# Later sum over partitions, and another order of entries in the two block-product GEMMs

## The chip, the cores and the metric

The kernel runs on one core of a Trainium2 chip, as one program. The metric is the time of one execution in microseconds on the device; the number that counts is the median of the runs. A core has a matrix engine (TensorE, PE in the profile), a vector engine (VectorE, DVE), a scalar engine (ScalarE, ACT), a general engine (GpSimd, POOL) and a queue engine (SyncE, SP). Each runs its own instructions in the order in which the program lists them, and waits on semaphores that the others raise.

## The reference

A stack of blocks on 512 tokens of 1024 features, all in float32: a bidirectional gated delta net with an MLP, a dilated window attention with an MLP, a final RMS norm, and then two more blocks (a Fourier and long-convolution mixer with a convolved feed-forward net on tokens and context, and a latent attention with such a feed-forward net on the 512 tokens). The change touches the GEMMs that follow a norm:

```
h = rmsnorm(x, g)            # x * rsqrt(mean(x^2) + eps) * g
mlp:       x + relu(h @ w1)**2 @ w2
conv ffn:  gate, val = split(modulate(h) @ w_up)
           x + g2 * (silu(dwconv3(gate)) * val) @ w_down
```

## The kernel before, in words

Features lie on the 128 partitions, 8 tiles of them (KD), and tokens along the free axis. Weights come in chunks of 128 x 1024, four in a ring. A product of float32 accuracy is made of three matmuls: ScalarE rounds a chunk to a high part (`split_high`, L208), GpSimd subtracts to get the low part (`split_low`, L214), and PE multiplies low by high, high by low and high by high (L278 to L280). There are two slots for high and low parts, so the split of chunk n waits until tile n - 2 is done. An output tile n takes chunk n: 24 matmuls of 512 columns, or 48 of 256, and one of four PSUM banks.

`LateNorm`: the GEMM starts on x times the gain, and the division by the root mean square is made when VectorE drains a tile. On ScalarE stand, in this order (`split_high_first`): the high parts of x (`high`), the split of chunk 1, the squares (`square`, L474), the split of chunk 2, the root (`root`, L375), and then the splits from chunk 3 on. VectorE adds the squares of the eight tiles (`add_squares`, L362), PE adds them over the partitions with a matmul of ones (`tensor`, L371), ScalarE takes the root, VectorE inverts it (`inverse`, L505 or L3212) and can then drain tile 0. `multiply_tiles` issues PE's part, with L371 behind tile 1. One stream runs in the stages gdn_in, window_in and mlp1 (`mlp_stage`), two in mix_in, ffn0, mla_in and ffn1. The stages follow one another with a barrier between.

`mlp_seven_stage` (mlp0) and `ffn_seven_stage` (ffn1) make the first output tiles in the plain way (six in mlp0, `WHOLE`; ten in ffn1, five gate and value pairs), and the rest in pairs j of two weight chunks by `SevenProducts`: seven products of half-size blocks (G1, G0, V1, S1, S2, S4, S3), 12 matmuls of 256 columns each, on weights G, V and their sums S and on token blocks (b10, b00, b11 plain; T1, T2, T4, T3 differences, called mixes). Every block and every weight sum needs a high part from ScalarE and a low part (`rest`, `low_sum`, `low_raw`, `low_s3`) from VectorE or GpSimd. PE's order in pair j is G1, G0, V1, S1, the S3 of pair j - 1, S2, S4. S2 adds into the bank of G0, so it waits until VectorE has read it out (`add_c11`, L3163), and S1, S2, S4 wait for their low parts on VectorE (`low_sum`, L3157). In pair 0, PE also waits for the remainders of the blocks (`ready`), and pair 1 waits for all of them. The order of each engine's entries in this turn from tiles to products is written out by hand.

```
for n in range(min(RING, g.whole)):
    tile(n, n, 0)
    if n == 1 and norm.late:
        norm.tensor(pe)
```

## Time and profile before

| | us |
|---|---|
| median of 3 runs | 3236.82 (3236.43 to 3240.74) |
| the profiled execution, its own time | 3245.98 |
| its span, first to last instruction | 3244.2 |
| PE busy | 3046.9 (94%) |
| VectorE, GpSimd, ScalarE busy | 1720.5, 1208.2, 1156.6 |

The mean clock that PE was granted is 0.963 of full speed; it has two levels, 1.2 and 2.4 GHz. Times in rows are microseconds from the start of the span. A duration of a matmul overlaps the next one's, so the distance between starts is what a matmul costs.

### The profile page before, as it was taken

The numbers are of one execution on the slowest core, as the hardware profiler recorded it, in microseconds if no ns is written. First come the engines' busy times: TensorE is split into PE (matmuls) and PEld (weight loads), VectorE is DVE, ScalarE is ACT, GpSimd is POOL, SyncE is SP. The second block draws the span as 40 slices with busy tenths as digits, with TensorE's granted clock in tenths as the row PEclk, the third lists the DMA queues.
The fourth block names the chain that finished last, engine by engine and source line by source line (L and its number), as shares of the span: only waits on it lengthen the run. The fifth ranks groups of instructions, "written<-read, shape, count | busy, mean of one in ns | idle before, by whom it ended". The sixth has DMA issues, their size and how long they took to land. (4 is left out here: it accounts for less than half of the span.)

```text
span 3244.2 us, 51107 instructions
## 1 busy us (share of the span) xinstructions
PE 3046.9 (94%) x19422; PEld 2460.3 (76%) x19422; DVE 1720.5 (53%) x2594; ACT 1156.6 (36%) x1905; POOL 1208.2 (37%) x642
## 2 busy tenths in 40 slices
PE   8988888999999989999898999999999979999998
PEld 6845666998878767888477788888888545589987
DVE  7835653762131535311577766555556666478731
ACT  4323433563231723222221332222223435345632
POOL 4432213664434024444122022222232147646643
PEclk9978989999999989999899999999999989999999
DMA  4326443222324022332212012122121112122322
GB/s 146 97 75 219 151 159 117 97 105 89 95 90 116 20 63 93 97 94 95 86 59 80 30 59 65 58 65 65 58 65 59 50 38 49 39 78 92 106 97 84
DMA packets 80218, 275.75 MB, mean 85 GB/s; under 512 B 9500, under 2 KB 12380, under 8 KB 79291
## 3 DMA queue, kind: packets, MB, share of 16 engines
q1 hardware_dynamic: 79771, 273.27, 26.2%
q8 instruction: 107, 1.75, 0.2%
q14 instruction: 52, 0.43, 0.0%
q10 hardware_dynamic: 288, 0.30, 0.0%
HBM read 263.54 MB, written 2.12 MB: 82 GB/s over the span
## 5 line engine op out<-in xcount | busy, mean ns | idle before, releaser
L214 POOL TENSOR_TENSOR weights_low<-weight_ring,weights_high 128x1024 fp32r<-128x1024 f32 x303 | 750.4, 2477 | 1441.0 <-ACT weights_high L208 1441.0
L208 ACT ACTIVATE weights_high<-weight_ring 128x1024 fp32r<-128x1024 f32 x317 | 333.9, 1053 | 631.3 <-PE bank L280 627.3
L278 PE MATMUL bank<-ffn_in_high,weights_low 128*128 128x512 f32 (+2 forms) x1176 | 399.0, 339 | 6.4 <-POOL weights_low L214 3.8
L279 PE MATMUL bank<-ffn_in_low,weights_high 128*128 128x512 f32 (+2 forms) x1176 | 398.5, 339 | 0.0
L280 PE MATMUL bank<-ffn_in_high,weights_high 128*128 128x512 f32 (+2 forms) x1176 | 398.2, 339 | 0.0
L278 PEld LDWEIGHTS bank<-ffn_in_high,weights_low 128*128 128x128 f32 x1176 | 222.9, 190 | 32.3 <-POOL weights_low L214 4.4
L279 PEld LDWEIGHTS bank<-ffn_in_low,weights_high 128*128 128x128 f32 x1176 | 223.0, 190 | 24.5
L280 PEld LDWEIGHTS bank<-ffn_in_high,weights_high 128*128 128x128 f32 x1176 | 222.0, 189 | 24.2
L634 DVE TENSOR_TENSOR mlp_down_low<-mlp_hidden,mlp_down_high 128x512 fp32r<-128x512 f32 x64 | 48.8, 764 | 285.3 <-ACT mlp_down_high L553 285.3
L278 PE MATMUL bank<-mlp_down_high,weights_low 128*128 128x512 f32 x496 | 193.1, 389 | 2.0 <-POOL weights_low L214 2.0
L279 PE MATMUL bank<-mlp_down_low,weights_high 128*128 128x512 f32 x496 | 193.0, 389 | 0.0
L280 PE MATMUL bank<-mlp_down_high,weights_high 128*128 128x512 f32 x496 | 192.9, 389 | 0.0
L634 DVE TENSOR_TENSOR ffn_in_low<-ffn_hidden,ffn_in_high 128x512 fp32r<-128x512 f32 (+1 forms) x44 | 61.3, 1416 | 142.5 <-ACT ffn_in_high L553 142.5
L553 ACT ACTIVATE mlp_down_high<-mlp_hidden 128x512 fp32r (+1 forms) x64 | 40.2, 631 | 231.0 <-PE bank L280 225.8
L278 PEld LDWEIGHTS bank<-mlp_down_high,weights_low 128*128 128x128 f32 x496 | 93.1, 188 | 21.9 <-issue 2.4
L280 PEld LDWEIGHTS bank<-mlp_down_high,weights_high 128*128 128x128 f32 x496 | 93.1, 188 | 19.2
L279 PEld LDWEIGHTS bank<-mlp_down_low,weights_high 128*128 128x128 f32 x496 | 93.1, 188 | 19.2
L278 PE MATMUL bank<-gdn_in_high,weights_low 128*128 128x512 f32 x248 | 98.6, 398 | 0.5 <-POOL weights_low L214 0.5
L278 PE MATMUL bank<-mlp_in_high,weights_low 128*128 128x512 f32 x248 | 97.3, 393 | 0.8 <-POOL weights_low L214 0.8
L280 PE MATMUL bank<-gdn_in_high,weights_high 128*128 128x512 f32 x248 | 98.1, 395 | 0.0
L279 PE MATMUL bank<-gdn_in_low,weights_high 128*128 128x512 f32 x248 | 98.1, 395 | 0.0
L279 PE MATMUL bank<-mlp_in_low,weights_high 128*128 128x512 f32 x248 | 96.5, 389 | 0.0
(791 smaller groups left out, 7905.3 us busy)
## 6 DMA issues: line engine op xcount, KB each, us to landing
weight_ring<-in_mod SPq DMA_DIRECT2D x96, 512.0 KB, 4.7
weight_ring<-in_ffn_up SPq DMA_DIRECT2D x88, 512.0 KB, 3.5
weight_ring<-in_mlp_up SPq DMA_DIRECT2D x64, 512.0 KB, 3.5
weight_ring<-in_mlp_down SPq DMA_DIRECT2D x64, 512.0 KB, 3.4
weight_ring<-in_ffn_down SPq DMA_DIRECT2D x44, 512.0 KB, 3.5
weight_ring<-in_gdn_in SPq DMA_DIRECT2D x32, 512.0 KB, 3.5
weight_ring<-in_dswa_in SPq DMA_DIRECT2D x27, 512.0 KB, 3.5
weight_ring<-in_fh_in SPq DMA_DIRECT2D x16, 512.0 KB, 3.4
```

What stands on the lines that cost most here:

```text
L208: act.activation(self.high[:, (g.s0 + at) % SPLIT, 0:g.floats], raw, ACT.Copy).then_inc(self.high_ready, 1)
L214: pool.tensor_tensor(self.low[:, slot, 0:g.floats], self.ring[:, (g.c0 + at) % RING, 0:g.floats], self.high[:, slot, 0:g.floats], ALU.subt ...
L278: pe.matmul(bank, wl, ah, start=start, stop=False)
L279: pe.matmul(bank, wh, al, start=False, stop=False)
L280: return pe.matmul(bank, wh, ah, start=False, stop=stop)
L553: last = act.activation(self.high[at % 2][:, :, lo:lo + tokens], src(k * self.kc, self.kc), ACT.Copy)
L634: last = dve.tensor_tensor(self.low[at % 2][:, :, lo:lo + tokens], src(k * self.kc, self.kc), self.high[at % 2][:, :, lo:lo + tokens], ALU ...
```

## The change

With one stream, L371 is issued behind tile 2 instead of tile 1 (also in mlp0's own code); with two streams it stays. In mlp0, ScalarE makes the squares before the split of chunk 1, and the high parts of S1, S2 and S4 in a row before it keeps product G1 (`keep_b`); VectorE makes the mix T1, then the inverse, then T2 and T4, while T3 goes to GpSimd; the weight sums stand behind tile 3 instead of tile 5, and pair 0's `add_c11` right behind the low parts of S1 and S2. In ffn1 the remainder of b00 moves from behind pair 3 to behind pair 2, that of T2 from VectorE to GpSimd, GpSimd makes the raw low parts of pair 0 before its remainders, and pair 0's `add_c11` stands ahead of the low part of S2. With `late_sums`, ffn1 keeps the wait of the sum S2 for the high part of S1, and mlp0 loses it.

```diff
--- before.py
+++ after.py
@@ -311,7 +311,7 @@
             norm.tensor(pe)
         for n in range(min(RING, g.whole)):
             tile(n, n, 0)
-            if n == 1 and norm.late:
+            if n == (1 if len(streams) > 1 else 2) and norm.late:
                 norm.tensor(pe)
         if beside:
             beside.tensor(pe)
@@ -2929,7 +2929,7 @@
     BLOCKS_OF = ("b10", "T4", "b00", "T1", "T2", "b11", "T3")
     UNIT = KH * P
 
-    def __init__(self, core, name, g, ctx, wide, first, pairs, blocks_high, blocks_low, kept, s3, banks, slots=None):
+    def __init__(self, core, name, g, ctx, wide, first, pairs, blocks_high, blocks_low, kept, s3, banks, slots=None, late_sums=False):
         self.core, self.g, self.pairs, self.wide = core, g, pairs, wide
         g.seven = self
         self.bh, self.bl = blocks_high, blocks_low
@@ -2945,7 +2945,7 @@
             w[self.S2], w[self.S4] = halves(shared, 1 - slot)
         self.sums = dict(zip((self.S1, self.S2, self.S4), [core.ps[b] for b in banks]))
         self.base = 2 * (first % 2)
-        self.s3, self.kept = s3, kept
+        self.s3, self.kept, self.late_sums = s3, kept, late_sums
 
     def signals(self, sems):
         (self.raw_high, self.raw_low, self.s_sums, self.s_high, self.s_low, self.s3_sum, self.s3_high, self.s3_low, self.products,
@@ -3075,7 +3075,7 @@
     def high_sum(self, act, j, w):
 
         self.slot_free(act, j, w)
-        act.wait_ge(self.s_sums, 3 * j + (3 if w != self.S1 else 2 if j else 1))
+        act.wait_ge(self.s_sums, 3 * j + (3 if w != self.S1 else 1 if self.late_sums and not j else 2))
         act.activation(self.wh[w], self.sums[w][:, :], ACT.Copy).then_inc(self.s_high, 1)
 
     def high_s3(self, act, j):
@@ -3137,7 +3137,7 @@
         dve.wait_ge(self.s_sums, 3 * j + 1)
         if j:
             dve.wait_ge(self.s_low, 3 * j - 1)
-        else:
+        elif self.late_sums:
             dve.wait_ge(self.s_high, 1)
         dve.tensor_tensor(self.sums[self.S2][:, :], self.sums[self.S1][:, :], self.raw(dve, j, False)[:, 0:self.UNIT], ALU.subtract) \
            .then_inc(self.s_sums, 1)
@@ -3252,6 +3252,9 @@
             def _(pool):
                 core.split_low(pool, up, up.ahead, WHOLE)
                 seven.low_raw(pool, 0)
+                pool.wait_ge(tokens_scaled, KD)
+                pool.wait_ge(mixed_ready, len(MIXES) - 1)
+                pool.tensor_tensor(raw["T3"], quarter(1, 1), quarter(0, 1), ALU.subtract).then_inc(mixed_ready, 1)
                 seven.sum_s3(pool, 0)
                 for j in range(N):
                     if j + 1 < N:
@@ -3302,8 +3305,9 @@
 
                 first_tile()
                 tile(1)
+                tile(2)
                 norm.tensor(pe)
-                for n in range(2, WHOLE):
+                for n in range(3, WHOLE):
                     tile(n)
                 for j in range(N):
                     if j == 1:
@@ -3340,8 +3344,8 @@
                 if not up.ahead:
                     core.split_high(act, up, 0, 0, 0)
                 norm.high(act)
+                norm.square(act)
                 core.split_high(act, up, 1, 1, 0)
-                norm.square(act)
                 core.split_high(act, up, 2, 2, 0)
                 scale_tokens()
                 norm.root(act)
@@ -3351,14 +3355,12 @@
                         round_block(MIXES[n - 3])
                 for w in (seven.G1, seven.G0, seven.V1):
                     seven.high_raw(act, 0, w)
-                seven.high_sum(act, 0, seven.S1)
+                for w in (seven.S1, seven.S2, seven.S4):
+                    seven.high_sum(act, 0, w)
                 for j in range(N + 2):
                     now, later = j < N, j + 1 < N
                     if now:
                         seven.keep_b(act, j)
-                    if j == 0:
-                        for w in (seven.S2, seven.S4):
-                            seven.high_sum(act, 0, w)
                     if later:
                         seven.high_raw(act, j + 1, seven.G1)
                     if j >= 2:
@@ -3395,9 +3397,8 @@
                 dve.sem_inc(up_drained, RING)
 
                 def mix(which):
-                    first, second = dict(T1=(quarter(0, 1), quarter(0, 0)), T2=(quarter(1, 1), raw["T1"]), T4=(quarter(1, 0), raw["T2"]),
-                                         T3=(quarter(1, 1), quarter(0, 1)))[which]
-                    if which in ("T2", "T4"):
+                    first, second = dict(T1=(quarter(0, 1), quarter(0, 0)), T2=(quarter(1, 1), raw["T1"]), T4=(quarter(1, 0), raw["T2"]))[which]
+                    if which != "T1":
                         dve.wait_ge(mixed_ready, MIXES.index(which))
                     dve.tensor_tensor(raw[which], first, second, ALU.subtract).then_inc(mixed_ready, 1)
 
@@ -3425,19 +3426,21 @@
                 norm.lows(dve)
                 norm.sums(dve, order)
                 dve.wait_ge(tokens_scaled, KD)
-                for which in MIXES:
-                    mix(which)
+                mix("T1")
                 norm.inverse(dve, order)
+                mix("T2")
+                mix("T4")
                 for n in range(WHOLE):
-                    if n == WHOLE - 1:
-                        seven.sum_s1(dve, 0)
                     tile(n)
                     if n < len(MIXES) - 1:
                         rest(MIXES[n])
-                seven.low_sum(dve, 0, seven.S1)
-                seven.sum_s2(dve, 0)
-                seven.sum_s4(dve, 0)
-                seven.low_sum(dve, 0, seven.S2)
+                    if n == WHOLE - 3:
+                        seven.sum_s1(dve, 0)
+                        seven.sum_s2(dve, 0)
+                        seven.sum_s4(dve, 0)
+                for w in (seven.S1, seven.S2):
+                    seven.low_sum(dve, 0, w)
+                seven.add_c11(dve, 0, hid[:, WHOLE, 0:H])
                 for j in range(N + 1):
                     now, later = j < N, j + 1 < N
                     gates, values = [hid[:, WHOLE + 2 * (j - 1) + x, :] if j else None for x in range(2)]
@@ -3451,7 +3454,7 @@
                         rectify(WHOLE + 2 * (j - 1), seven.c12_added, j)
                     if later:
                         seven.sum_s2(dve, j + 1)
-                    if now:
+                    if now and j:
                         seven.add_c11(dve, j, hid[:, WHOLE + 2 * j, 0:H])
                     if later:
                         seven.sum_s4(dve, j + 1)
@@ -3499,7 +3502,7 @@
         kept = core.xc[:, 0:6, :]
         last = 6 + (FIRST - 1) % 2
         seven = SevenProducts(core, "ffn1_seven", up, ctx, H, FIRST, N, block_high, block_low, kept, pick[:, :, :].rearrange("p a n -> p (a n)"),
-                              (13 - last, last, 5), [f[:, KH * H:KH * H + SevenProducts.UNIT] for f in flat])
+                              (13 - last, last, 5), [f[:, KH * H:KH * H + SevenProducts.UNIT] for f in flat], True)
         rows = RowsGemm(core, "ffn1_down", down, [(tiles_of(hid, 0, T), core.x, T, mod.gate(1, 0))], ctx, 2,
                         both=[t[:, :, 0:H].rearrange("p k t -> p (k t)")[:, 0:2 * T].rearrange("p (b k t) -> p b k t", b=2, k=1) for t in parts[0]])
         GATE = core.ps[4]
@@ -3516,8 +3519,8 @@
             MIXES = ("T1", "T2", "T4", "T3")
             PLAIN = ("b10", "b00", "b11")
             ROUNDED = (*PLAIN, *MIXES)
-            RESTS = ("b10", "b00", "T4", "T1", "T2", "T3")
-            POOL_RESTS = ("b11",)
+            RESTS = ("b10", "b00", "T4", "T1", "T3")
+            POOL_RESTS = ("T2", "b11")
             index = SevenProducts.BLOCKS_OF.index
 
             @block.sync
@@ -3542,10 +3545,10 @@
                 core.split_low(pool, up, 8, 9)
                 mix("T4")
                 core.split_low(pool, up, 9, up.whole)
+                seven.low_raw(pool, 0)
                 for name in POOL_RESTS:
                     pool.wait_ge(block_rounded, ROUNDED.index(name) + 1)
                     pool.tensor_tensor(block_low[index(name)], blocks[name], block_high[index(name)], ALU.subtract).then_inc(pool_rests, 1)
-                seven.low_raw(pool, 0)
                 mix("T3")
                 seven.sum_s3(pool, 0)
                 for j in range(N):
@@ -3747,16 +3750,17 @@
                             scale_tokens(k)
                     if m == 2:
                         rest("b10")
+                        rest("b00")
                     if m == FIRST - 2:
                         dve.wait_ge(hidden_ready, FIRST - 1)
                         seven.sum_s1(dve, 0)
-                        for name in ("b00", "T4", "T1"):
+                        for name in ("T4", "T1"):
                             rest(name)
                 seven.low_sum(dve, 0, seven.S1)
                 dve.wait_ge(hidden_ready, FIRST)
                 seven.sum_s2(dve, 0)
                 seven.sum_s4(dve, 0)
-                rest("T2")
+                seven.add_c11(dve, 0, gate_halves(0)[0])
                 seven.low_sum(dve, 0, seven.S2)
                 for j in range(N + 1):
                     now, later = j < N, j + 1 < N
@@ -3770,7 +3774,7 @@
                         more_taps(j - 1)
                     if later:
                         seven.sum_s2(dve, j + 1)
-                    if now:
+                    if now and j:
                         seven.add_c11(dve, j, gate_halves(j)[0])
                     if later:
                         seven.sum_s4(dve, j + 1)
```

## Rows read from the trace of the kernel before

**Rows 1.** The page: span, busy time of each engine.

```profile
span 3244.2 us, 51107 instructions
...
PE 3046.9 (94%) x19422; PEld 2460.3 (76%) x19422; DVE 1720.5 (53%) x2594; ACT 1156.6 (36%) x1905; POOL 1208.2 (37%) x642
```

**Rows 2.** The list of PE's waits, whole run (engine, line, releaser: total us, times, longest).

```profile
PE bank L604 <- ACT mixer_out_high L553: 4.4, 1, 4.4
...
PE bank L371 <- DVE mlp_hidden L362: 3.3, 2, 1.8
```

**Rows 3.** PE's timeline, window_in, 928 to 932 us (start, duration, instruction [idle before]).

```profile
928.48 0.39 PE L280 MATMUL bank<-window_in_high,weights_high 128*128 128x512 f32 x1
930.62 1.12 PE L371 MATMUL bank<-window_qkv,ones 128*128 128x512 f32 x2 [1.75 <-DVE window_qkv L362]
...
931.81 0.39 PE L279 MATMUL bank<-window_in_low,weights_high 128*128 128x512 f32 x1
```

**Rows 4.** ScalarE's timeline, window_in: root, split of chunks 3 and 4.

```profile
931.78 0.69 ACT L375 ACTIVATE rstd<-bank,eps 128x512 f32<-128x512 f32 x1 [6.67 <-PE bank L371]
932.37 1.05 ACT L208 ACTIVATE weights_high<-weight_ring 128x1024 fp32r<-128x1024 f32 x1
937.38 1.06 ACT L208 ACTIVATE weights_high<-weight_ring 128x1024 fp32r<-128x1024 f32 x1 [3.96 <-PE bank L280]
```

**Rows 5.** GpSimd's timeline, window_in: lower parts of chunks 2 and 3.

```profile
925.18 3.57 POOL L214 TENSOR_TENSOR weights_low<-weight_ring,weights_high 128x1024 fp32r<-128x1024 f32 x1 [2.14 <-ACT weights_high L208]
933.49 2.42 POOL L214 TENSOR_TENSOR weights_low<-weight_ring,weights_high 128x1024 fp32r<-128x1024 f32 x1 [4.74 <-ACT weights_high L208]
```

**Rows 6.** ScalarE's timeline, mlp0: the squares, now behind the split of chunk 1.

```profile
563.62 3.70 ACT L474 ACTIVATE mlp_hidden<-x 128x2048 f32<-128x2048 f32 x2
```

**Rows 7.** GpSimd's timeline, mlp0: lower parts of chunks 1 and 2.

```profile
563.79 2.40 POOL L214 TENSOR_TENSOR weights_low<-weight_ring,weights_high 128x1024 fp32r<-128x1024 f32 x1 [9.51 <-ACT weights_high L208]
568.34 3.57 POOL L214 TENSOR_TENSOR weights_low<-weight_ring,weights_high 128x1024 fp32r<-128x1024 f32 x1 [2.15 <-ACT weights_high L208]
```

**Rows 8.** VectorE's timeline, mlp0: the adds of squares, the four mixes, the inverse.

```profile
567.35 6.37 DVE L362 TENSOR_TENSOR mlp_hidden<-mlp_hidden 128x2048 f32<-128x2048 f32 x3 [3.45 <-ACT mlp_hidden L474]
573.63 7.07 DVE L3402 TENSOR_TENSOR mlp_hidden<-mlp_hidden 128x1024 f32<-128x1024 f32 x4
580.63 3.34 DVE L3212 RECIPROCAL rstd<-rstd 128x512 f32<-128x512 f32 x1
```

**Rows 9.** PE's timeline, mlp0: starts of tile 1, of product S2, of pair 1.

```profile
566.24 0.39 PE L278 MATMUL bank<-mlp_blocks_high,weights_low 128*128 128x256 f32 x1 [0.78 <-POOL weights_low L214]
...
607.68 0.55 PE L2999 MATMUL bank<-mlp_blocks_high,weights_low 128*128 128x256 f32 x1 [4.00 <-issue]
...
612.75 0.28 PE L2999 MATMUL bank<-mlp_blocks_high,mlp_seven_weights_low 128*128 128x256 f32 x1
```

**Rows 10.** VectorE's timeline, mlp0: the sum that product S2 waits for.

```profile
607.16 0.42 DVE L3163 TENSOR_TENSOR mlp_hidden<-bank,mlp_kept 128x256 f32<-128x256 f32 x1
```

**Rows 11.** Windows (us, each engine's busy us, PE's granted clock, DMA): mlp0 around S2.

```profile
608.00:613.00 5.00, 5.00 (x27) 5.00 (x27) 2.74 (x5) 2.33 (x5) 3.96 (x3) 0.55 0.00 0
```

**Rows 12.** Windows: behind the wait of 4.4 us in mixer_out.

```profile
1851.00:1856.00 5.00, 5.00 (x15) 3.99 (x16) 5.00 (x4) 2.19 (x3) 2.73 (x1) 0.66 0.21 84
```

**Rows 13.** PE's timeline, ffn1: starts of products S1, S2 and of pair 1.

```profile
2940.13 0.38 PE L2999 MATMUL bank<-ffn_blocks_high,weights_low 128*128 128x256 f32 x1 [3.16 <-DVE weights_low L3157]
...
2946.25 0.55 PE L2999 MATMUL bank<-ffn_blocks_high,weights_low 128*128 128x256 f32 x1 [3.39 <-DVE ffn_padded L3163]
...
2951.11 0.28 PE L2999 MATMUL bank<-ffn_blocks_high,ffn_seven_weights_low 128*128 128x256 f32 x1
```

**Rows 14.** Windows: ffn1 around S1 and S2.

```profile
2941.00:2946.00 5.00, 1.86 (x9) 1.57 (x8) 4.96 (x7) 3.27 (x8) 2.74 (x2) 0.50 0.59 210
```

**Rows 15.** VectorE's timeline, ffn1: a bias add under GpSimd, three remainders.

```profile
2919.01 3.95 DVE L3696 TENSOR_SCALAR ffn_padded<-ffn_padded,ffn_shift 128x256 f32<-128x256 f32 x2
...
2928.09 4.60 DVE L3720 TENSOR_TENSOR ffn_blocks_low<-ffn_hidden,ffn_blocks_high 128x1024 fp32r<-128x1024 f32 x3
```

## The prediction

> **What bounds the kernel now.** I read the page first: PE is busy 94% of a 3244.2 us span and no other engine passes 53% [rows 1]. So time is saved or lost where PE stands still, or where its clock falls. The list of PE's waits comes next. The matmul that adds squares over partitions (L371) waits for VectorE's adds: 3.3 us in the two MLPs together [rows 2], 1.75 us in window_in [rows 3]; the three rows of the one-stream stages, gdn_in's among them, make 6.8 us. In mlp0 PE waits 4.00 us before product S2 [rows 9], in ffn1 3.16 us before S1 and 3.39 us before S2 [rows 13]. The windows then show what follows such waits: the granted clock falls. These places are what the change touches, about 17 us of waiting together. Last I read each engine's timeline around them, because the question is what gets late when something else moves.
>
> **The stages with one stream (gdn_in, window_in, mlp1).** Only one thing changes: L371 is issued after tile 2 instead of after tile 1. window_in stands for all three.
>
> Before: tile 1's last matmul starts at 928.48; L371 starts at 930.62 and tile 2's second matmul at 931.81 [rows 3]. The pitch of a 512-column matmul is 0.235 us there, so tile 1 gives way at 928.71, tile 2 begins in effect at 931.58, its 24 matmuls take 5.6 us, and tile 3 begins at 937.2 (ScalarE's split of chunk 4, which waits for the end of tile 2, starts at 937.38 [rows 4]). From the end of tile 1 to the start of tile 3: 8.5 us.
>
> After: tile 2 needs the lower part of chunk 2, which GpSimd ends at 925.18 + 3.57 = 928.75 [rows 5], so it starts at about 928.85, and the 1.75 us wait is gone. It ends at 934.45 and L371 follows at once. But what is queued behind L371? ScalarE takes the root, and behind the root in its in-order program stands the split of chunk 3; GpSimd's lower part of chunk 3 waits for that split, and tile 3 for the lower part. Before, this chain ran beneath tile 2. Now tile 2 is over and PE has nothing to do. Its length is in the rows: L371 at 930.62, root at 931.78, split at 932.37 [rows 4], lower part from 933.49 to 935.91 [rows 5], which is 5.3 us. Tile 3 starts at 934.45 + 5.35 = 939.8 instead of 937.2: **2.6 us later**, 2.7 with the slower first matmul after a wait. PE is idle some 4.3 us of it, L371 itself being about 1.1. The rest of such a stage has PE busy throughout, so nothing gives the time back. VectorE's inverse also moves, but bank 0 is first wanted by tile 4, a whole tile later. Three stages: **+8.1 us**. Bounds per stage: 1.75 us less than no loss (if the chain did not hold PE at all), and 3.5 if GpSimd's part took 3.57 as in the other of its rows [rows 5].
>
> **mlp0, its first tiles.** Here ScalarE's squares (3.70 us [rows 6]) also move ahead of the split of chunk 1. The lower part of chunk 1 begins 3.7 us later than 563.79, so at about 567.4, and now under VectorE's adds, which begin 0.95 us earlier, at 566.4. A lower part alone takes 2.40; the one issued under the adds takes 3.57 [rows 7, 8]. I take 3.57, the nearest row: tile 1 starts at 571.0 instead of 566.24 [rows 9], an idle of 5.6 us where there was 0.78. Then tile 1 and tile 2 take 5.76 each (48 matmuls of 0.12), L371 stands at 582.6, and tile 3 5.35 later, at 587.9. Before, tile 2 began at 574.73 and tile 3 at 580.5. **+7.4 us** at tile 3. VectorE now does the inverse (3.34) and two mixes (2 x 1.77 [rows 8]) behind the root; bank 0 is free about 9.6 us after L371, while tile 4 wants it 11.1 us after, so this stays hidden by 1.5 us. T3's mix on GpSimd takes VectorE's 1.77 us away and hides behind the raw lower parts.
>
> **mlp0, the turn into the products.** Before, tile 5 gives way to the products at about 597.8, and pair 1 starts at 612.75 [rows 9]: 15.0 us for six products of 1.44, because S2 waits for a sum that VectorE does at 607.16, behind pair 1's sums [rows 10], and then runs at 0.55 of the clock [rows 11]. After, that sum stands right behind the lower parts of S1 and S2, and S4's high part is made before product G1 ends. By the same durations the six products run without a wait, 8.65 us, and pair 1 waits 0.4 for T3's remainder: 9.05. **-5.95 us.** mlp0 without the clock: +1.45. Bounds: -5.95 could be -4 if the remainder of T3 came 2 us later.
>
> **ffn1.** Two streams, so L371 does not move. S1 waits for VectorE, which does three remainders (4.60 us, [rows 15]) before pair 4. One of them, b00, moves to a point two tiles earlier, and T2 goes to GpSimd; but b00's cost comes with it, before pair 3, so pair 4 starts where it did and S1 still starts at about 2940.1. From there VectorE has S2's and S4's sums (1.3 us) and then adds c11 at once, so S2 follows S1. The clock falls here at 2940.4 and stays at half for 10 us; with the wait for S2 gone I give it 3.4 us at half, which costs 1.7. Pair 1 by PE alone: 2940.1 + 4.3 + 1.7 = 2946.1; T3's remainder, which follows the sums of pair 1, holds it until about 2947.5. Before it was 2951.11 [rows 13]. **-3.6 us.** Bounds: GpSimd now has T2 and b11 and T3 in a row under pair 4. The two bias adds of a pair took 3.95 us when GpSimd was at work [rows 15], 0.62 otherwise; another 2.2 us of it would leave -1.4. If no clock falls, -5.
>
> The Trainium skill (SBUF — State Buffer, on the port pair that VectorE and GpSimd share) says that the pair is an exclusive lock, and that of two such instructions the later one fully blocks until the first is done. The 3.57 of rows 7 and the 3.95 of rows 15 agree. By that rule the worst of pair 4's bias adds would be two waits of a whole 2.4 us GpSimd operation, 4.8 us, and ffn1 would gain nothing; by the row the change of 1.74 to 3.95 leaves a gain of 1.4.
>
> **The clock.** Sum so far: 8.1 + 1.45 - 3.6 = +6 us. PE waits of 1.5 to 1.8 us before L371 left the clock at 2.4 GHz. After the 4.43 us wait in mixer_out it was 0.66 over five us, so 3.4 us at 1.2 GHz, and 1.7 us of work lost [rows 2, 12]; after mlp0's 4.00 us it was 0.55 over five us [rows 11], 4.5 us at half, 2.3 lost. In the list of waits set against the clock, each of the twelve waits of 3.5 us or more has a stretch at half in it or right behind. The change makes five new waits of this size: one in each of three stages and two in mlp0 (4.3 and 5.6 us). At 2.1 us each: **+10.5 us**. Bounds: 5 x 1.0 and 5 x 2.9. In ffn1 the loss from the clock was the window at 0.50 [rows 14], counted above.
>
> **Sum.** +16.5 us. The profiled execution took 3245.98 us, 1.8 more than its span, and would take 3262; the median of the runs is 3236.82, and I forecast **3253 us**. What a measurement of this kernel can tell from no change is 0.2%, 6.5 us.
>
> **The rivals.**
> - *The clock hardly falls, and both turns gain at the upper bound.* +6 with two falls instead of five (4) and ffn1 at -5: +8, so 3245; with no fall, 3241. For it: waits of 2.31 us left the clock up in places. Against it: twelve of twelve. Chance 0.13.
> - *Chunk 3 does not hold PE (the other side).* If the lower part of chunk 3 were ready when L371 ends, the three stages gain 1.75 each and mlp0's tile 3 comes at 583 instead of 587.9. Then -5.2 + 2.5 - 5.95 - 3.6 + 2 for one clock fall = -10, so 3227. It decides when the split of chunk 3 is done 2.4 us before tile 2 ends; the order in ScalarE's program, root first, speaks against it. Chance 0.04.
> - *VectorE and GpSimd collide in ffn1 and mlp0.* One collision of 2.2 us at pair 4's bias adds (3.95 in place of 1.74) and one of 1.4 at pair 1's sums take ffn1's 3.6, and T3's remainder in mlp0 comes 2 us late: +5.6, so 3259. For it, 3.95 against 0.62. Chance 0.12.
> - The forecast, 3246 to 3260 by itself: chance 0.71.
>
> **How the numbers follow.** Faster by over 0.2% (below 3230.3) is the second rival: 0.04. Within 0.2% (to 3243.3) is the lower half of the first: 0.07. Slower: 0.89. The range leaves out the second rival, the lowest of the first, and the highest of the third together with three clock falls of 2.9: 3242 to 3262.
>
> **What would show it.** After the change: L371 without a wait in the one-stream stages, and in each a PE wait of about 4.3 us at tile 3 put down to GpSimd's L214, the clock at half behind it; in mlp0 tile 1 waiting 5.6 us; the product part of mlp0 9 us from tile 5 to pair 1; ffn1's S2 right behind S1. It is wrong if tile 3 starts right behind L371, or if the clock stays at 2.4 GHz behind these waits.

## The result: slower, and by more than the sum said

The changed kernel takes 3261.24 us (median of 6 runs, 3257.47 to 3274.45), the kernel before 3237.49 beside it: ratio 1.0076, 95% interval [1.0063, 1.0090]. The forecast was 3253 with a range from 3242 to 3262, so the median lies just inside the range; but by the ratio the loss is 24.6 us (0.0076 x 3237.49; the interval is 20 to 29), where the sum said 16.5. The profiled execution took 3268.2 us, 1.8 more than its span.

The page of the changed kernel, span and PE, against [rows 1]:

```profile
span 3266.4 us, 51108 instructions
...
PE 3051.6 (93%) x19422; PEld 2467.7 (76%) x19422; DVE 1729.0 (53%) x2592; ACT 1155.9 (35%) x1905; POOL 1212.5 (37%) x644
```

Its list of PE's waits, against [rows 2] (engine, line, releaser: total us, times, longest). PE's waits for a lower part on GpSimd were 9.5 us in the kernel before, the longest 2.0:

```profile
PE bank L278 <- POOL weights_low L214: 29.2, 11, 4.9
...
PE bank L2999 <- issue: 6.5, 3, 2.4
...
PE bank L2999 <- DVE weights_low L3157: 4.9, 3, 3.2
```

L371 no longer appears there for the one-stream stages. What stands in its place is the row with 29.2. PE's timeline of the changed kernel, in order of time: tile 3 of gdn_in, tiles 1 and 3 of mlp0 with L371 between them, mlp0's products V1, S1 and pair 1, L371 and tile 3 of window_in, tile 3 of mlp1:

```profile
33.11 0.50 PE L278 MATMUL bank<-gdn_in_high,weights_low 128*128 128x512 f32 x1 [4.14 <-POOL weights_low L214]
...
568.87 0.58 PE L278 MATMUL bank<-mlp_blocks_high,weights_low 128*128 128x256 f32 x1 [4.86 <-POOL weights_low L214]
...
582.57 1.02 PE L371 MATMUL bank<-mlp_hidden,ones 128*128 128x512 f32 x2
587.74 0.58 PE L278 MATMUL bank<-mlp_blocks_high,weights_low 128*128 128x256 f32 x1 [4.15 <-POOL weights_low L214]
...
611.65 0.36 PE L2999 MATMUL bank<-mlp_blocks_high,mlp_seven_weights_low 128*128 128x256 f32 x1 [2.20 <-issue]
...
614.70 0.39 PE L2999 MATMUL bank<-mlp_blocks_high,weights_low 128*128 128x256 f32 x1 [1.38 <-DVE weights_low L3157]
...
621.22 0.39 PE L2999 MATMUL bank<-mlp_blocks_high,mlp_seven_weights_low 128*128 128x256 f32 x1 [1.95 <-issue]
...
946.09 1.02 PE L371 MATMUL bank<-window_qkv,ones 128*128 128x512 f32 x2
951.25 0.50 PE L278 MATMUL bank<-window_in_high,weights_low 128*128 128x512 f32 x1 [4.14 <-POOL weights_low L214]
...
1254.87 0.80 PE L278 MATMUL bank<-mlp_in_high,weights_low 128*128 128x512 f32 x1 [4.15 <-POOL weights_low L214]
```

Five new waits, four of them forecast at 4.3 us and one at 5.6; the forecast said that the products of mlp0 would run without one until 0.4 before pair 1. The windows behind them, that of gdn_in first, show the granted clock (third number from the right); for window_in, 0.66 over five us is 3.4 us at 1.2 GHz:

```profile
33.00:38.00 5.00, 4.89 (x14) 3.91 (x15) 3.89 (x7) 0.01 (x1) 2.44 (x2) 0.66 0.58 177
569.00:574.00 5.00, 5.00 (x25) 5.00 (x26) 4.78 (x3) 2.07 (x4) 3.13 (x1) 0.54 0.48 126
587.00:592.00 5.00, 4.26 (x24) 4.26 (x25) 4.93 (x3) 1.01 (x2) 3.03 (x2) 0.66 0.58 140
952.00:957.00 5.00, 5.00 (x16) 3.91 (x16) 1.38 (x2) 0.00 (x0) 1.55 (x1) 0.66 0.66 210
1255.00:1260.00 5.00, 5.00 (x13) 3.92 (x14) 4.56 (x6) 0.00 (x0) 2.14 (x1) 0.53 0.69 197
```

To see where the time went I subtracted, stage by stage, the times between the waits that open two successive stages in the two traces (after less before; gdn_in from the start of the span, mlp0 and mlp1 with their down projections, ffn1 without): gdn_in +4.1, window_in +4.2, mlp1 +4.9, mlp0 +13.8, ffn1 +0.8, in all +27.8. The other stages, which the change doesn't touch, took 5.6 us less in the profile of after; in one of them, the gated delta net behind gdn_in, the profile of before took 363.1 us and the others, this one among them, 353.1 to 357.5. So the single profile of before is a long one, and the span's difference (22.2) isn't the change's worth. A second profile of the changed kernel (e8, below) gave mlp0 +6.5 and the rest alike.

**The one-stream chain** is as forecast. ScalarE and GpSimd in window_in of the changed kernel, against [rows 4, 5]:

```profile
947.15 0.69 ACT L375 ACTIVATE rstd<-bank,eps 128x512 f32<-128x512 f32 x1 [10.36 <-PE bank L371]
947.74 1.99 ACT L208 ACTIVATE weights_high<-weight_ring 128x1024 fp32r<-128x1024 f32 x2
```

```profile
948.86 4.70 POOL L214 TENSOR_TENSOR weights_low<-weight_ring,weights_high 128x1024 fp32r<-128x1024 f32 x2 [8.43 <-ACT weights_high L208]
```

ScalarE sat idle 10.36 us before the root, with the split of chunk 3 queued behind it. From L371 at 946.09 to tile 3 at 951.25 is 5.16 us (5.3 to 5.35 in the sum).

**mlp0's turn.** VectorE of the changed kernel, two remainders, then the sums of S1, S2 and S4:

```profile
596.74 3.43 DVE L3407 TENSOR_TENSOR mlp_blocks_low<-mlp_hidden,mlp_blocks_high 128x1024 fp32r<-128x1024 f32 x1
...
601.80 2.31 DVE L3407 TENSOR_TENSOR mlp_blocks_low<-mlp_hidden,mlp_blocks_high 128x1024 fp32r<-128x1024 f32 x1
...
605.73 2.90 DVE L3133 TENSOR_TENSOR bank<-weight_ring 128x512 f32<-128x512 f32 x1
608.66 0.70 DVE L3142 TENSOR_TENSOR bank<-bank,weight_ring 128x512 f32<-128x512 f32 x1
609.40 0.70 DVE L3151 SCALAR_TENSOR_TENSOR bank<-bank,weight_ring 128x512 f32<-128x512 f32 x1
```

GpSimd at the same time (lower part of chunk 5; mix T3), and ScalarE (the three high sums, the keeping of G1):

```profile
596.22 2.87 POOL L214 TENSOR_TENSOR weights_low<-weight_ring,weights_high 128x1024 fp32r<-128x1024 f32 x1 [6.19 <-ACT weights_high L208]
...
605.22 2.85 POOL L3257 TENSOR_TENSOR mlp_hidden<-mlp_hidden 128x1024 f32<-128x1024 f32 x1
```

```profile
609.46 1.82 ACT L3079 ACTIVATE weights_high<-bank 128x512 fp32r<-128x512 f32 x3 [7.46 <-DVE bank L3142]
611.15 0.39 ACT L3091 ACTIVATE mlp_kept<-bank 128x256 f32<-128x256 f32 x1
```

VectorE ends the sum of S1 at 608.63. G1 started at 606.40 and PE was free for V1 at 609.45, but the three high sums end at 611.28 and the keeping of G1 at 611.54. So V1 and S1 had to wait for what follows that sum, and pair 1 came 14.82 us after the start of G1 (14.99 in the kernel before, where it waited 4.00 before S2 [rows 9]). The 4.00 was taken away and three others, 5.5 us together, came for it. VectorE's timeline of the kernel before, the same two remainders and the sum of S1:

```profile
588.09 3.43 DVE L3406 TENSOR_TENSOR mlp_blocks_low<-mlp_hidden,mlp_blocks_high 128x1024 fp32r<-128x1024 f32 x1
...
593.15 2.31 DVE L3406 TENSOR_TENSOR mlp_blocks_low<-mlp_hidden,mlp_blocks_high 128x1024 fp32r<-128x1024 f32 x1
...
598.79 0.69 DVE L3133 TENSOR_TENSOR bank<-weight_ring 128x512 f32<-128x512 f32 x1
```

The two long remainders aren't new. The long sum is: 2.90 us behind GpSimd's mix T3, which began half a microsecond before it, where it took 0.69. Nor had VectorE less time before G1: from ScalarE's root to G1 it was 22.83 us before (574.93 to 597.76) and is 22.77 now (583.63 to 606.40), because the wait at tile 3 holds PE back as far as the later root holds VectorE.

**ffn1.** VectorE and GpSimd of the changed kernel, against [rows 15]: the remainders of b10 and b00, and pair 3's bias adds.

```profile
2937.96 6.17 DVE L3723 TENSOR_TENSOR ffn_blocks_low<-ffn_hidden,ffn_blocks_high 128x1024 fp32r<-128x1024 f32 x2
...
2945.02 3.93 DVE L3699 TENSOR_SCALAR ffn_padded<-ffn_padded,ffn_shift 128x256 f32<-128x256 f32 x2
```

```profile
2937.31 2.40 POOL L3538 TENSOR_TENSOR ffn_hidden<-ffn_hidden 128x1024 f32<-128x1024 f32 x1
2939.67 3.38 POOL L214 TENSOR_TENSOR weights_low<-weight_ring,weights_high 128x1024 fp32r<-128x1024 f32 x1
2943.01 3.38 POOL L3538 TENSOR_TENSOR ffn_hidden<-ffn_hidden 128x1024 f32<-128x1024 f32 x1
```

PE's timeline there, against [rows 13]: products G1, S1, S2, pair 1.

```profile
2957.30 0.39 PE L2999 MATMUL bank<-ffn_blocks_high,ffn_seven_weights_low 128*128 128x256 f32 x1 [1.91 <-POOL ffn_seven_weights_low L3114]
...
2965.76 0.38 PE L2999 MATMUL bank<-ffn_blocks_high,weights_low 128*128 128x256 f32 x1 [3.15 <-DVE weights_low L3157]
...
2968.52 0.58 PE L2999 MATMUL bank<-ffn_blocks_high,weights_low 128*128 128x256 f32 x1 [0.32 <-DVE weights_low L3157]
...
2974.50 0.35 PE L2999 MATMUL bank<-ffn_blocks_high,ffn_seven_weights_low 128*128 128x256 f32 x1 [2.38 <-issue]
```

S2 follows S1 by 2.76 us where it was 6.12; the wait of 3.39 is down to 0.32. But the stage starts 22.7 us later in this trace, so G1 is 2.5 us later in the stage and S1 3.0 us later: the gain behind S1 is spent before it.

### The profile page after: what moved, and what is told of

Same layout as the page of the kernel before. It is cut to its first block and busy times, and to the rows that moved or that the text cites. A ratio compares the mean times of both kernels' runs of the same rounds, so it can differ in the third digit from the quotient of the medians.

```text
span 3266.4 us, 51108 instructions
## 1 busy us (share of the span) xinstructions
PE 3051.6 (93%) x19422; PEld 2467.7 (76%) x19422; DVE 1729.0 (53%) x2592; ACT 1155.9 (35%) x1905; POOL 1212.5 (37%) x644
```

## The experiments

Ratios are to the kernel before, run beside each on the same chip.

| kernel | median us | ratio [95%] |
|---|---|---|
| e1, L371 alone | 3253.31 | 1.0044 [1.0028, 1.0060] |
| e2, mlp0 alone | 3250.11 | 1.0035 [1.0023, 1.0046] |
| e3, ffn1 alone | 3240.89 | 1.0011 [1.0003, 1.0020] |
| e4, L371 later, split of chunk 3 first | 3239.56 | 1.0003 [0.9995, 1.0012] |
| e5, mlp0's turn alone | 3236.75 | 0.9990 [0.9981, 0.9999] |
| e6, the same, keeping of G1 first | 3236.79 | 0.9992 [0.9983, 1.0001] |
| e7, ffn1 alone, b00 in its old place | 3236.07 | 0.9990 [0.9981, 0.9999] |
| e8, the changed kernel again | 3266.13 | 1.0084 [1.0069, 1.0100] |
| e9, combined | 3231.55 | 0.9980 [0.9969, 0.9991] |
| e10, changed, split of chunk 3 first | 3247.37 | 1.0030 [1.0019, 1.0041] |
| e11, changed, squares back | 3255.29 | 1.0055 [1.0039, 1.0071] |
| e12, changed, T3's mix on VectorE | 3265.65 | 1.0077 [1.0062, 1.0093] |
| e13, e9 with mlp0's L371 behind tile 1 | 3230.46 | 0.9973 [0.9961, 0.9985] |
| e14, changed, keeping of G1 first | 3262.99 | 1.0072 [1.0057, 1.0087] |
| e15, changed, mlp0's L371 behind tile 1 | 3255.35 | 1.0053 [1.0037, 1.0068] |

**e1 to e3: the parts alone.** e1 is before with this line, e2 the change's edits in mlp0 alone, e3 those in ffn1 alone.

```diff
-            if n == 1 and norm.late:
+            if n == (1 if len(streams) > 1 else 2) and norm.late:
```

> The kernel before with one line changed: in gdn_in, window_in and mlp1 the matmul L371 stands behind tile 2. Theory (the chain root, split, lower part of chunk 3 stands uncovered behind L371): each of the three stages shows one wait of 4.1 us at tile 3 in place of the 1.7 us before L371, is 2.6 us longer by that and 1.7 to 2.3 more by the clock, and mlp0 and ffn1 are as before: +13 us, ratio 1.0040. Rival (the moved matmul costs little, and the 24 us came from the two block-product GEMMs): under +4 us.

> The kernel before with mlp0 alone as in the changed one (its own L371, the squares ahead of chunk 1, the new order of the turn). Theory: the first tiles lose 7 us and the clock some 5, and the turn gains almost nothing, because three new waits of 2.2, 1.4 and 2.0 us stand where one of 4.0 stood: mlp0 12 us longer, +12, ratio 1.0037. Rival (my forecast for the stage, the turn gains 6 us): +5.6. Second rival (mlp0 was longer only through the phase of the clock in that execution): its waits are as before and the stage within 3 us.

> The kernel before with ffn1 alone as in the changed one. Theory (b00's remainder two tiles earlier runs under GpSimd's work, takes 3 us instead of 1.2, and delays pair 3, with it ScalarE's raw high parts and G1, and S1): S1 starts 3 us later than before counted from the start of the stage, the wait for S2 is gone, the stage is 0 to +2 us: ratio 1.0000 to 1.0006. Rival (my forecast): S1 starts where it did and the stage is 3.6 us shorter, 0.9989.

By the ratios the parts cost 14.2, 11.3 and 3.6 us, 29 together, about the whole within the intervals. The profile of e1 has gdn_in +3.8, window_in +5.3, mlp1 +5.0, that of e3 ffn1 +0.8. The theories of e1 and e3 hold in their profiles, with e1's waits of 4.1 us at tile 3 and e3's S1 3.0 us later in the stage. e2's holds only in its ratio. Its mlp0 is, step for step, that of the changed kernel, and its profile has the waits of 5.49 and 4.15 us at tiles 1 and 3, but of the three waits expected in the turn only one, 1.03 us before pair 1: the turn takes 9.83 us, and mlp0 is at +6.5, less than the ratio says. Its ten executions lie between 3240.32 and 3255.19, and the profiled one (3244.16) is the third shortest.

**e4: the order behind L371.** L371 stands behind tile 2 in all four one-stream stages, but ScalarE splits chunk 3 before the root.

```diff
             first[2]()
+            if len(norm.streams) == 1:
+                self.split_high(act, g, SPLIT + 1, SPLIT + 1, 0)
+                norm.root(act)
+                return SPLIT + 2
             norm.root(act)
```

> The kernel before with L371 behind tile 2 in the four one-stream stages, mlp0 too, and with the split of chunk 3 moved ahead of the root on ScalarE; nothing else changed. Theory (it is the order root, then split, that makes the late matmul dear): tile 3 starts right behind L371, the 1.5 to 1.8 us waits before L371 are gone, and no clock falls there: 6 us shorter than before, ratio 0.9980. Rival (the late matmul is dear by itself, through the root and the inverse that VectorE needs before it can drain tile 0): a wait of 3 to 4 us at tile 4 in each of the four stages, +10 us or more.

By the ratio nothing is gained, where the theory had 6 us. window_in and mlp1 are at -1.8 and -1.7 us as it said, but mlp0 is at +0.3 and gdn_in at +4.3. In mlp0 the wait before L371 is gone, but the turn, still in its old order, takes 16.39 us instead of 14.99. In gdn_in the reason stands one tile further on. PE's and ScalarE's timeline of e4, gdn_in:

```profile
44.63 0.79 PE L282 MATMUL bank<-gdn_in_high,weights_low 128*128 128x512 f32 x1 [3.63 <-POOL weights_low L214]
```

```profile
40.62 0.60 ACT L861 ACTIVATE conv<-bank 128x512 f32 x1
41.11 1.05 ACT L208 ACTIVATE weights_high<-weight_ring 128x1024 fp32r<-128x1024 f32 x1
```

There ScalarE's split of chunk 5 is queued behind the first tile's silu, which waits for VectorE's drain and taps, and so for the root; in the kernel before that silu stood at 36.28. A later root is free only where nothing that feeds PE is queued behind what uses it.

**e5 and e6: mlp0's turn alone** (L371 and the squares as before); in e6 ScalarE also keeps G1 ahead of the three high sums.

> The kernel before with only the turn of mlp0 changed (order of the mixes, T3's on GpSimd, early weight sums, high parts of S1, S2, S4 in a row, early c11); L371 stays behind tile 1 and the squares behind the split of chunk 1. Theory (the turn gains where VectorE has its drains done in time, and loses it where it has not): here the root comes early, so VectorE is ahead; V1 waits about a microsecond for the keeping of G1, which stands behind the three high sums, and pair 1 starts 9 to 11 us after tile 5 instead of 15: stage 4 to 6 us shorter, ratio 0.9982 to 0.9988. Rival (the new order is no better by itself, the three small waits of the changed kernel are its own): 14 to 15 us, stage as before, ratio 1.0000.

> The run before this one, with the keeping of product G1 ahead of the high parts of S1, S2 and S4 on ScalarE. Theory: the wait of V1 is gone, and S1 waits for its low part instead if that is late; 0.5 to 1 us shorter than the run before this one. Rival: no difference, because S1's low part was the one that ended last.

Both have mlp0 at -3.8 us, and 11.14 us from G1 to pair 1. By its profiles the turn as such is a gain, of the size of the lower bound (-4), and the place of the keeping makes no difference. The ratios say 3.2 and 2.6 us, and e6's interval just reaches 1.

**e7: ffn1 with the remainder of b00 back in its old place**, the rest of ffn1's edits kept.

```diff
                         rest("b10")
-                        rest("b00")
...
-                        for name in ("T4", "T1"):
+                        for name in ("b00", "T4", "T1"):
```

> ffn1 alone changed, but with b00's remainder in its old place behind pair 3. Theory (the early remainder under GpSimd's work is what costs the 3 us): G1 starts without the 1.9 us wait, pair 3 is 3 us earlier, but three remainders stand ahead of pair 4 again less one that went to GpSimd, so S1 starts about 1.5 us later than before and pair 1 1.5 to 3 us earlier; stage 1.5 to 3 us shorter than before, ratio 0.9991 to 0.9995. Rival (c11 early is worth nothing, since T3's remainder ends last anyway): stage within 0.5 us of before.

ffn1 is at -2.5 us, 3.3 us better than e3 by the profiles. (The down projection behind it took 1.2 us less than before in e7, but also in e6, which doesn't touch ffn1, and not in e3; I don't count it.) In e7 the three remainders run in a row in 4.60 us and pair 4's bias adds take 1.74, both as before. S1 starts 0.3 us earlier in the stage than before, not 1.5 later as the theory said.

**e8: the changed kernel again**, for a second profile.

> The changed kernel once more, for a second profile. Theory: the waits of 4.1 us at tile 3 and of some 5 us at mlp0's tile 1 are there again; the turn of mlp0 takes between 10 and 15 us, less where the clock fell for longer during the tiles and VectorE caught up; sum of the touched stages +20 to +27 us over before, median 24 us over before. Rival (the first profile was typical in all places): the turn at 14.8 us again.

Its span is 3259.0, with the same waits in the other stages (gdn_in +4.0, window_in +4.3, mlp1 +4.3, ffn1 +0.8), but mlp0 is at +6.5 and from G1 to pair 1 it took 9.84 us, so the touched stages are at +19.8. By the ratio e8 is 27 us slower than before; its profiled execution (3260.83) is the fastest of its four. VectorE and GpSimd of e8, the same steps as above:

```profile
596.70 1.22 DVE L3407 TENSOR_TENSOR mlp_blocks_low<-mlp_hidden,mlp_blocks_high 128x1024 fp32r<-128x1024 f32 x1
...
604.61 1.78 DVE L3133 TENSOR_TENSOR bank<-weight_ring 128x512 f32<-128x512 f32 x1
```

```profile
597.44 2.75 POOL L214 TENSOR_TENSOR weights_low<-weight_ring,weights_high 128x1024 fp32r<-128x1024 f32 x1 [7.45 <-ACT weights_high L208]
```

The two VectorE timelines agree within 0.04 us up to this remainder. In e8 the clock was at half for longer behind tile 3's wait (0.61 over the seven us from 588, against 0.81), so PE ended tile 3 later, ScalarE split chunk 5 at 596.30 instead of 595.08, and GpSimd began after VectorE instead of 0.5 us before it. Then G1 is 1.2 us later and VectorE's sums are 2.2 us earlier. The other profiles with the wait at tile 3 and the new turn agree. Where the turn is long (changed, e12, e14), the clock over the same seven us (from 4.4 us behind the root) is 0.81 and chunk 5 is split 11.4 us after the root; where it is short (e8, e2, e11), the clock is 0.61, 0.61 and 0.65 and the split comes 12.4 to 12.7 us after the root. A slower clock goes with a shorter turn, though no run sets the clock by itself.

**e9: what paid, together.** e6's turn, e7's ffn1, and e4's order in window_in, mlp1 and mlp0 but not in gdn_in.

> The parts of the change that paid, and none of those that cost: L371 behind tile 2 with the split of chunk 3 ahead of the root in window_in, mlp1 and mlp0 but not in gdn_in, the turn of mlp0 with keep_b ahead of the three high sums, ffn1 with b00's remainder in its old place. If the parts add up: window_in -1.8 and mlp1 -1.7 us as alone, mlp0 -1.7 for the wait before L371 and -3.8 for the turn, ffn1 with its down part -3.7: -12.7 us, ratio 0.996. Rival, that they get in each other's way in mlp0, where the later root moves VectorE's drains by a tile and lets them meet GpSimd's work at the turn: mlp0 gains nothing, -7 us, ratio 0.998.

Faster by 6.5 us, less than the 12.7 of the parts. gdn_in is at 0.0, window_in -1.8, mlp1 -1.7, ffn1 -2.5, as in the parts alone; mlp0 is at -1.3, not at -5.5. PE's timeline of e9, mlp0, start of tile 4:

```profile
577.87 0.36 PE L282 MATMUL bank<-mlp_blocks_high,weights_low 128*128 128x256 f32 x1 [2.56 <-DVEq L3425]
```

Tile 4 wants bank 0 and VectorE hasn't drained it: here the later root holds VectorE and no wait at tile 3 holds PE; with this wait of 2.56, from the root to G1 it is still only 21.34 us.

**e10 to e12: one step of the changed kernel put back at a time**: the split of chunk 3 ahead of the root, the squares behind the split of chunk 1, the mix T3 on VectorE.

> The changed kernel with one order in ScalarE's program turned round, the split of chunk 3 ahead of the root in the four one-stream stages. Theory, that the root ahead of the split is what makes L371 behind tile 2 dear: window_in and mlp1 go from +4.2 and +4.9 us against the kernel before to -1.8 each, mlp0 loses its wait of 4.15 us at tile 3 and the clock fall behind it (1.7), gdn_in stays at +4 (its drains run late then): 18 us less than the changed kernel, ratio to the kernel before 1.002. Rival, that the later matmul itself costs, by later drains: the waits come back at tiles 4 and 5, ratio over 1.005.

> The changed kernel with ScalarE's squares in mlp0 back behind the split of chunk 1. Theory, that in mlp0 the squares ahead of the split are a pure cost, since L371 now stands behind tile 2 and its squares have time: PE's wait of 4.86 us at tile 1 and the clock fall with it (1.7 to 2) go, 6 us less than the changed kernel, ratio 1.006. Rival, that the squares behind the split make VectorE's adds late enough for L371 to wait and for the root to be late: 2 us or less gained, ratio 1.007 to 1.0085.

> The changed kernel with mix T3 of mlp0 back on VectorE, behind mix T4, and the rest of the change kept. Theory, that T3's mix on GpSimd blocks the ports while VectorE makes the sum of S1 (2.90 us where 1.78 without) and by it delays the high sums on ScalarE and keep_b behind them: from the start of G1 to pair 1 10 to 11.5 us where the changed kernel's profile has 14.8, ratio 1.0065. Rival, that GpSimd's lower part of chunk 5 over VectorE's remainder (3.43 us) is what delays it, whatever T3 does: the sequence stays at 14 us or more, and VectorE's 1.77 us more make the drain of tile 0 late, ratio 1.008 or more.

e10: 1.0030, between the two numbers; against the changed kernel's 1.0076 that is 15 us back. window_in and mlp1 are at -1.7 each (from +4.2 and +4.9). In mlp0 the wait at tile 3 is gone, but tile 4 waits 2.58 us for VectorE, and from G1 to pair 1 it takes 16.16. e11: as the theory had it (ratio 1.0055), mlp0 at +2.7, without the wait of 4.86; the turn is 3.7 us shorter than in the changed kernel's profile too, which the theory hadn't foreseen. e12: the theory fell by the turn, and its rival held; the interval of the ratio holds the numbers of both. With T3 on VectorE the sum of S1 takes 0.69 but starts 0.82 us after G1, and the turn takes 14.10.

**e13 to e15: is it VectorE's backlog?** e13 is e9 with L371 of mlp0 behind tile 1 again; e14 and e15 are the changed kernel with only the keeping of G1 first, and with only L371 of mlp0 back behind tile 1.

```diff
                 tile(1)
-                tile(2)
                 norm.tensor(pe)
-                for n in range(3, WHOLE):
+                for n in range(2, WHOLE):
```

> The combined kernel with L371 of mlp0 back behind tile 1 and the root ahead of the split of chunk 3 there; window_in, mlp1, ffn1 and mlp0's turn as in it. Theory, that VectorE's chain from the root to its drains is what the later matmul delays in mlp0: the wait of 2.56 us at tile 4 and the half-clock stretch behind it go, mlp0 at -3.8 us against the kernel before instead of -1.3, ratio 0.9972. Rival, that the wait of 1.8 us before L371 comes back and takes it all: mlp0 at -1.3 again, ratio 0.998.

> The changed kernel with one step moved on ScalarE in mlp0, the keeping of G1 ahead of the three high sums. Theory, that in the changed kernel the three high sums wait for VectorE and hold G1's bank by it: PE's waits before V1 (2.20) and half of that before S1 go, from the start of G1 to pair 1 12 to 13 us instead of 14.8, ratio 1.0068. Rival, that the sequence goes by VectorE's backlog alone (drains, remainders, sums, in one row since the root): the wait only moves from V1 to S1, still 14 us or more, ratio 1.0075 or more.

> The changed kernel with L371 of mlp0 back behind tile 1; squares still ahead of the split of chunk 1. Theory, that the later root both empties PE at tile 3 and makes VectorE late for the products: the 4.15 us at tile 3, a half-clock stretch (1.7) and 3.7 us of the 14.8 from G1 to pair 1 go, while the 4.86 us at tile 1 stays; mlp0 from +13.7 to about +4, ratio 1.0046. Rival, that the long sequence comes from GpSimd's work and the order of the sums and not from the root: it stays at 14 us or more, mlp0 at +8, ratio 1.006.

e14: V1 no longer waits, S1 does. PE's timeline of e14:

```profile
613.08 0.49 PE L2999 MATMUL bank<-mlp_blocks_high,weights_low 128*128 128x256 f32 x1 [3.56 <-DVE weights_low L3157]
```

The turn takes 14.09: the wait only moved, as e14's rival said, and its ratio, 1.0072, lies between the two. e15: 11.14, with no wait in the turn before pair 1's 1.76; mlp0 is at +2.4, and the ratio, 1.0053, again lies between the two numbers. The end of VectorE's sum of S1, less the start of G1, puts all profiles with the new turn in order:

| kernel | sum of S1 ends after G1 starts | G1 to pair 1 |
|---|---|---|
| e8, e2 | -1.23, -1.24 | 9.84, 9.83 |
| e11 | -0.97 | 11.14 |
| e15, e13, e5, e6 | -0.45 to -0.43 | 11.14 or 11.15 |
| e9 | -0.17 | 11.14 |
| e12 | +1.51 | 14.10 |
| e14 | +2.23 | 14.09 |
| changed | +2.23 | 14.82 |
| e10 | +3.72 | 16.16 |

The late root alone doesn't decide: e11, e8 and e2 have it as well and are short. Against e15 the changed kernel has VectorE just 0.4 us later after the root, and that is enough to change who comes first. In e15 VectorE begins the third remainder at 593.68, ahead of GpSimd's lower part at 593.96, and it takes 1.21 us; in the changed kernel it begins at 601.80, behind GpSimd's at 601.62, and takes 2.31. Then the sum of S1 begins 1.2 us ahead of T3's mix in e15 (1.78 us), and 0.5 us behind it in the changed kernel (2.90 us).

e13 is the fastest version, 0.9973, 8.7 us less than before; its interval overlaps e9's, so that the early matmul in mlp0 is better than e9's late one isn't shown. Its profile has mlp0 at -0.6 and not at -3.8: its four waits are within 0.03 us of e6's, but the clock fell in three places where it had stayed up (last section).

## Why the prediction was right or wrong

**L371 in the one-stream stages: right.** Forecast 2.7 us and 2.1 for the clock in each, 14.4 for three; measured 4.1, 4.2 and 4.9 in the profile, 13.3, and 14.2 by e1's ratio. The reason given, the root ahead of the split of chunk 3 in ScalarE's program, is shown by e4 and e10: turned round, window_in and mlp1 gain 1.7 to 1.8 us each. The rival that ends faster stated exactly this condition. In gdn_in it alone doesn't help (e4); the prediction had seen of VectorE's part only bank 0.

**The clock: right.** Five new waits, each with half-clock behind it. In window_in the stage lost 4.2 us: 2.5 are there when tile 3 starts (24.1 us into the stage, 21.6 before), and 1.7 come behind it, where the clock is at half for 3.4 us (2.1 forecast). The Trainium skill (TensorE: Matmul & The Clock Gate, Terms) puts the loss at about the time at half times one half; that is 1.7 here, and the trace agrees.

**mlp0's first tiles: right in kind.** Tile 1 waited 4.86 (5.6), tile 3 4.15 (4.3), and G1 starts 10.7 us later in the stage (11.5 in e8 and e2), where tile 3's 7.4 and two falls of the clock at 2.1 made 11.6. e11 takes the squares back and gains 6.8 us by the ratio (0.0021 x 3237), about the wait and its clock. Its profile can't size this alone, since its turn isn't that of either profile of the changed kernel: mlp0 is 11.1 us shorter than in the first and 3.8 than in e8.

**mlp0's turn: wrong.** The step that failed is "S4's high part is made before product G1 ends. By the same durations the six products run without a wait, 8.65 us", for -5.95. The three high sums ended 1.8 us after PE was free for V1, and the six products waited 3.6 us before V1 and S1 and 1.95 before pair 1. The sum followed VectorE after the late root only to bank 0 and found 1.5 us to spare there. It didn't go on: four drains, three remainders and three sums stand in one row behind that root, and what follows them is wanted from V1 on. Nor are all durations the same: the sum of S1, moved to a time when GpSimd works on T3's mix, took 2.90 us instead of 0.69. (The two long remainders, 3.43 and 2.31, are in the kernel before too.) The third rival had a collision here, but at T3's remainder and of 2 us. So the turn gave -0.2 in this profile, and -5.2 in those of e8 and e2. With the root early (e5) it gives -3.8. e14 and e12 exclude the keeping and the mix as the only cause; what decides is where VectorE's row stands against G1 and against GpSimd's, by some tenths of a microsecond. How often the long turn comes in the executions that weren't profiled isn't known.

**ffn1: wrong.** "b00's cost comes with it, before pair 3, so pair 4 starts where it did" failed. The two remainders took 6.17 us under GpSimd's mix and lower part, where one alone took 2.84 before: 3.3 us for b00, where it took 1.2 in its old place. Pair 3, and with it the split weights for G1, came later, and S1 3.0 us. e7 shows it: with b00 back the stage is 3.3 us shorter and 2.5 under before, of 3.6 forecast, inside its bounds (-1.4, -5). The price stood in the bound of the bias adds, 2.2 us, only for another place.

The Trainium skill (SBUF — State Buffer, two separate sides) says of the shared port pair that an instruction of VectorE with two inputs in SBUF blocks until GpSimd's is done, if GpSimd's reads SBUF and started first. The trace agrees: the remainder of 596.74 began behind GpSimd's part, which ended at 599.09, and was done 1.08 us later, at 600.17; alone it takes 1.22.

**The sum.** Mis-sized by the turn (5.8 us in one profile, 0.8 in the other two) and ffn1 (4.4): 16.5 becomes 22 to 27, and 24.6 was measured. The first profile's mlp0 holds 3.2 us more that no term had: the clock fell behind pair 1 (0.83 over the ten us from 621) and in the down projection (0.91 over the twenty from 745), and in e8 in neither place. The range reaches 3262 only by the third rival, whose collisions were set at other places, so that the median lies inside it is in part luck.

## What to carry to other kernels

When a step is moved later on one engine, follow every queue behind its consumers to the next point at which PE needs them, not only to the first buffer; here the root fed ScalarE's next split, VectorE's drains, and behind them the sums and, in gdn_in, ScalarE's later splits. Before an instruction with two SBUF inputs is moved on VectorE, look what GpSimd does at its new time, and price it at what such a row took under GpSimd; here 0.4 us more or less decided who came first. Profile a kernel with such a place more than once. Try the parts of a reordering alone: kernels of its useful steps, with one order turned round, are 6 to 9 us faster than before (e9, e13), where the whole is 25 slower.

## What the runs showed of the hardware

The clock can fall behind far shorter waits than the prediction counted, and not each time. mlp0 of e6 and of e13 have the same waits of 2.3 us at its start, 1.7 before pair 1, and 2.0 in its down projection. Windows of ten us around them, e6 and then e13 (granted clock third from the right):

```profile
547.00:557.00 10.00, 7.62 (x52) 6.47 (x50) 6.88 (x11) 7.78 (x11) 1.73 (x1) 1.00 0.18 54
597.00:607.00 10.00, 8.27 (x69) 8.09 (x69) 9.25 (x12) 6.25 (x13) 6.26 (x5) 1.00 0.30 104
727.00:737.00 10.00, 8.00 (x36) 6.29 (x35) 2.06 (x2) 3.16 (x4) 5.17 (x2) 1.00 0.27 87
```

```profile
547.00:557.00 10.00, 7.66 (x49) 7.25 (x48) 6.67 (x10) 7.96 (x11) 1.92 (x1) 0.83 0.18 54
597.00:607.00 10.00, 8.24 (x57) 8.06 (x56) 8.06 (x12) 4.92 (x10) 5.18 (x4) 0.83 0.30 107
728.00:738.00 10.00, 8.00 (x29) 6.12 (x28) 2.33 (x3) 3.31 (x5) 5.16 (x2) 0.83 0.28 83
```

0.83 over ten us is 3.4 us at half, 1.7 lost at most, three times. e13's mlp0 is 3.2 us longer than e6's; the 5.1 us of the clock are more than enough for it. It may also be a reason why single profiles of this kernel differ by some us in stages that no edit touches; I haven't traced one of those. What decides whether it falls behind a wait of 2 us stays open.
